# A two-block transformer kernel: modulation columns moved into the state-space stage, one weight bank fetched early, expert slots by one-hot products

## Time and profile before

| | |
|---|---|
| median of 3 runs | 5024.47 us (5023.44 to 5026.74) |
| profiled execution | 5026.53 us, its span 5024.3 us |
| PE busy | 4302.4 us (86%) |
| DVE busy | 3027.8 us (60%) |
| ACT busy | 1993.8 us (40%) |
| POOL busy | 292.2 us (6%) |
| DMA | 700.93 MB, mean 140 GB/s |

### The profile page before, as it was taken

The page is one execution under the profiler, slowest core; times in us unless marked ns, Lnnn a source line. Parts: engine busy times, 40 slices in busy tenths (PEclk is TensorE's granted clock), DMA queues, the critical chain, the costliest instruction groups (busy, mean ns, idle before and its releaser), DMA issues. The chain is left out here.

```text
span 5024.3 us, 60591 instructions
## 1 busy us (share of the span) xinstructions
PE 4302.4 (86%) x21370; PEld 3341.1 (66%) x21370; DVE 3027.8 (60%) x3938; ACT 1993.8 (40%) x3109; POOL 292.2 (6%) x197
## 2 busy tenths in 40 slices
PE   7999699999675987999799999997597399999960
PEld 5777489888564865888555555555476278787740
DVE  6676455555465763444555555556654489888856
ACT  3344233333112543322233333333321277777743
POOL 0000110000000000000100000000000311111112
PEclk9999799999787998999899999998799699999985
DMA  4443411111563325222600000008443388888957
GB/s 170 144 147 129 151 52 39 39 39 44 170 195 130 109 86 180 70 68 65 196 13 13 13 19 13 13 5 258 171 137 108 122 312 316 314 319 331 392 202 285
DMA packets 345002, 700.93 MB, mean 140 GB/s; under 512 B 70816, under 2 KB 227488, under 8 KB 326432
## 3 DMA queue, kind: packets, MB, share of 16 engines
q1 hardware_dynamic: 312096, 608.98, 34.7%
q0 software_dynamic: 14848, 50.36, 2.7%
q10 hardware_dynamic: 17920, 39.85, 2.4%
HBM read 585.02 MB, written 194.56 MB: 155 GB/s over the span
## 5 line engine op out<-in xcount | busy, mean ns | idle before, releaser
L2189 DVE TENSOR_REDUCE a_part<-a_pA 128x1 f32<-128x1024 f32 (+1 forms) x384 | 360.8, 953 | 390.6 <-PE a_pA L2090 390.5
L2123 PE MATMUL a_pO<-a_PT,a_V 128*128 128x512 f32 x1152 | 587.7, 592 | 0.0
L2159 ACT ACTIVATE a_PT<-a_pB 128x512 f32<-128x512 f32 x576 | 343.9, 597 | 579.7 <-PE a_pB L2113 579.7
L2112 PE MATMUL a_pB<-a_QA,a_KH 128*128 128x512 f32 x576 | 458.0, 795 | 0.7 <-ACT a_QA L2151 0.7
L955 DVE TENSOR_REDUCE a_maxima<-a_pS 128x1 f32<-128x512 f32 x256 | 176.6, 690 | 177.3 <-PE a_pS L863 176.7
L3205 DVE TENSOR_TENSOR e_gate_low<-e_gate_w,e_gate_high 128x4096 fp32r<-128x4096 f32 x48 | 212.1, 4418 | 64.9 <-ACT e_gate_high L3137 64.6
L895 PE MATMUL a_pO<-a_V,a_PT 128*128 128x128 f32 x2048 | 249.4, 275 | 0.3 <-DVE a_PT L968 0.3
L895 PEld LDWEIGHTS a_pO<-a_V,a_PT 128*128 128x128 f32 x2048 | 243.4, 192 | 6.0 <-DVE a_PT L968 0.6
L2090 PE MATMUL a_pA<-a_KH,a_QA 128*128 128x512 f32 (+1 forms) x640 | 203.8, 385 | 50.4 <-DVE a_part L2189 30.4
L2123 PEld LDWEIGHTS a_pO<-a_PT,a_V 128*128 128x128 f32 x1152 | 205.6, 188 | 42.7 <-issue 1.0
L930 ACT ACTIVATE a_PT<-a_pT 128x512 f32<-128x512 f32 x128 | 69.5, 595 | 413.3 <-PE a_pT L881 413.3
(11 more groups left out here) (529 smaller groups left out, 9600.7 us busy)
## 6 DMA issues: line engine op xcount, KB each, us to landing
e_gate_w<-in_moe_w_gate SPq DMA_DIRECT2D x49, 2048.0 KB
e_up_w<-in_moe_w_up SPq DMA_DIRECT2D x48, 2048.0 KB, 13.4
e_down_w<-in_moe_w_down SPq DMA_DIRECT2D x47, 2048.0 KB
between_yb<-e_Y SPq DMA_DIRECT2D x47, 512.0 KB, 7.9
between_x<-m_X SPq DMA_DIRECT2D x32, 512.0 KB, 3.0
r_W<-in_w_ada SPq DMA_DIRECT2D x8, 2048.0 KB, 22.3
between_yb<-a_zeros SPq DMA_DIRECT2D x31, 512.0 KB, 10.4
between_tv<-p_OV SPq DMA_DIRECT2D x16, 576.0 KB, 2.8
```

The costliest lines, as they stand in the source:

```text
L2112: pe.matmul(pB[t % 2][:], KH[g][:, tile], QA1[i % 2][:, heads, :], start=True, stop=False)
L2123: pe.matmul(pO[u % 2][:], V1[:, j, u % HKV, :], PT[:, t % RING, :], start=j == 0, stop=j == KT2 - 1).then_inc(S["o_ps"], 1)
L2159: act.activation(PT[:, t % RING, :], pB[t % 2][:], ACT.Exp, scale=scale).then_inc(S["p_ready"], 1)
L2189: dve.tensor_reduce(part[:, h, r % (NG2 // G4):r % (NG2 // G4) + 1], src, AX_X, ALU.max).then_inc(S["maxed"], 1)
```

## The change

- `modulations` is gone. Its work is in `s5`: piece p is multiplied in turn h = p + 1, between `states(h + 1, 0..3)` and `outputs(h)`, and turned after `outputs(h)`, through two more uses of the banks `pW`. ACT moves row and columns and issues the 2 MB load of the next piece; there is one buffer for pieces. The silu is made in turn 0: a tanh on ACT behind the first load, three operations on DVE behind `scan(0)`. Bias and gains are made by DVE after the last scan.
- Bank 0 of `w_in_2` is loaded by SP during tile 4 of `mix_1` into a tensor that both stages share.
- The scatter to `slots` is gone. The slots are now a tensor on chip, made as a sum of 32 products of one-hot matrices: `in_row` (which row of its block a pair has) by `in_block` (which block, times the token number). The weights `gate` and `up` of the first block are loaded by SP inside `dispatch`, before its end. The DVE operations of the places and of the blocks change order.
- `experts` has no `IDX` loads. POOL gathers from the slots on chip, in an unrolled loop, and waits for `t_ps` itself.

```diff
-def s5(nc, I, D, C):
+def s5(nc, I, D, C, M):
+        ada_w = k.sb("ada_w", [P, KC, BANK])
+        FIRST_PIECE = 2
+        def piece_of(h):
+            return h - FIRST_PIECE if FIRST_PIECE <= h < FIRST_PIECE + PIECES else None
+        def uses_before(h):
+            return USES * h + 2 * max(0, min(h - FIRST_PIECE, PIECES))
...
+            for dst, name in ((cc, "c2"), (b_col, "b_ada_col"), (g1, "g1")):
+                sp.dma_start(dst[:], I[name]).then_inc(S["c_vectors_loaded"], 16)
...
+            def modulation_row(h):
+                p, n = piece_of(h), uses_before(h) + USES
+                if p == 0:
+                    pe.wait_ge(S["cs_ready"], 1)
+                weights_free(n)
+                pe.wait_ge(S["ada_loaded"], 16 * (p + 1))
+                for c in range(KC):
+                    mm = pe.matmul(pW[n % 2][:], both[:, c].rearrange("p x y -> p (x y)"), ada_w[:, c, :], start=c == 0, stop=c == KC - 1)
+                mm.then_inc(S["w_ps"], 1)
+            def modulation_columns(h):
+                n = uses_before(h) + USES + 1
+                pe.wait_ge(S["w_moved"], n)
+                for m in range(4):
+                    tr = pe.transpose(pW[n % 2][:, m * P:(m + 1) * P], row[:, m * P:(m + 1) * P], C["ident"][:])
+                tr.then_inc(S["w_ps"], 1)
...
                     for j in range(4):
                         states(h + 1, j)
+                    if piece_of(h + 1) is not None:
+                        modulation_row(h + 1)
                 pe.wait_ge(S["products_1"], h + 1)
                 outputs(h)
+                if h + 1 < TURNS and piece_of(h + 1) is not None:
+                    modulation_columns(h + 1)
...
+            def load_piece(p):
+                src = I["w_ada"].rearrange("(k p) n -> p k n", p=P)[:, :, p * BANK:(p + 1) * BANK]
+                act.dma_start(ada_w[:], src).then_inc(S["ada_loaded"], 16)
+            def move_row(h):
+                n = uses_before(h) + USES
+                act.wait_ge(S["w_ps"], n + 1)
+                act.activation(row[:], pW[n % 2][:], ACT.Copy).then_inc(S["w_moved"], 1)
+                if piece_of(h) + 1 < PIECES:
+                    load_piece(piece_of(h) + 1)
...
                     move_weights(h + 1)
+                    if piece_of(h + 1) is not None:
+                        move_row(h + 1)
                 move_outputs(h)
+                if h + 1 < TURNS and piece_of(h + 1) is not None:
+                    move_columns(h + 1)
+                if h == 0:
+                    load_piece(0)
+                    act.wait_ge(S["c_vectors_loaded"], 48)
+                    act.activation(half_c[:], cc[:], ACT.Tanh, scale=0.5).then_inc(S["tanh_done"], 1)
...
 # mix_1, SP
+                if 4 <= i < 4 + EARLY:
+                    load_projection(i - 4)
...
 # project_2, SP
-            for n, (lo, hi) in enumerate(BANKS2):
+            for n in range(EARLY, len(BANKS2)):
...
 # dispatch, SP
+            sp.wait_ge(S["first_known"], 1)
+            first = sp.value_load(M["block_expert"][0:1, 0:1], min_val=0, max_val=NE - 1)
+            for n in ("gate", "up"):
+                src = I["moe_w_" + n].rearrange("e (p k) n -> p e (k n)", p=P)
+                sp.dma_start(M["W"][n][0][:].unsqueeze(1), src[:, ds(first, 1), :]).then_inc(S["w_loaded"], 16)
+            sp.wait_ge(S["w_loaded"], 32)
...
 # dispatch, PE
+            pe.wait_ge(S["tokens_in"], 1)
+            for q in range(4):
+                pe.wait_ge(S["rows_in"], q + 1)
+                for j in range(8 * q, 8 * q + 8):
+                    mm = pe.matmul(ps[:, 0:NBT], in_row[:, j, :], in_block[:, j, :], start=j == 0, stop=j == 2 * NT - 1)
+            mm.then_inc(S["listed"], 1)
...
 # dispatch, DVE, behind the places and blocks
+            do(dve.tensor_scalar(of_block[:], dest[:], 1 / P, 0.5 / P - 0.5, ALU.mult, ALU.add))
+            do(dve.tensor_scalar(of_block[:], of_block[:], ROUND, None, ALU.add))
+            do(dve.tensor_scalar(of_block[:], of_block[:], ROUND, None, ALU.subtract))
+            do(dve.scalar_tensor_tensor(of_row[:], of_block[:], -float(P), dest[:], ALU.mult, ALU.add))
+            tt(in_block[:], bcast(flat(of_block).unsqueeze(2), shape), bcast(blocks_c[:].unsqueeze(1), shape), ALU.is_equal)
             for n in range(2):
+                d = dve.tensor_tensor(in_block[:, n * NT:(n + 1) * NT, :], in_block[:, n * NT:(n + 1) * NT, :],
+                                      bcast(token[:].unsqueeze(2), [P, NT, NBT]), ALU.mult)
+            for q in range(4):
+                dve.tensor_tensor(in_row[:, js, :], bcast(flat(of_row)[:, js].unsqueeze(2), [P, 8, P]), bcast(rows[:].unsqueeze(1), [P, 8, P]),
+                                  ALU.is_equal).then_inc(S["rows_in"], 1)
+            do(dve.tensor_copy(M["slots"][:], ps[:, 0:NBT]))
-                for t in range(NT):
-                    pool.indirect_dma_start(out=D["slots"], out_offset=bass.IndirectOffsetOnAxis(ap=M["dest"][:, n, t:t + 1], axis=0),
-                                            in_=token[:, t:t + 1], in_offset=None).then_inc(S["scattered"], 16)
...
 # experts, SP
-            load_indices(tile_at(0))
-            load_indices(tile_at(1))
-            load("gate", tile_at(0))
-            load("up", tile_at(0))
...
 # experts, POOL
+            for i in range(NB + 1):
+                if i >= 2:
+                    pool.wait_ge(S["t_ps"], i - 1)
+                pool.indirect_dma_start(out=XG[i % 2][:], out_offset=None, in_=D["h"],
+                                        in_offset=bass.IndirectOffsetOnAxis(ap=M["slots"][:, i:i + 1], axis=0)).then_inc(x_loaded[i % 2], 16)
```

More of the change, by code:

```diff
@@ L1062, in s5 @@
         Y = [k.sb(f"Y{b}", [P, HG, NCH]) for b in range(2)]
+        ada_w = k.sb("ada_w", [P, KC, BANK])
+        cc, half_c = (k.sb(n, [P, KC, 2]) for n in ("cc", "half_c"))
+        both = k.sb("both", [P, KC, 2, P // 2])
+        row = k.sb("row", [P, BANK])
+        columns = k.sb("columns", [P, PIECES, 4, 2])
+        b_col, g1 = k.sb("b_col", [P, NMOD * KC]), k.sb("g1", [P, KC])
         pW = [k.ps(f"pW{b}") for b in range(2)]
@@ L1288, in waiting_sp, with mix_1 @@
     return wait
-def mix_1(nc, I, D, C):
+def mix_1(nc, I, D, C, M):
     with ExitStack() as ctx:
@@ L1368, in tile @@
                     load(Tile(t.i + 2, t.b, t.n + 1))
-            tiles(sp, NT, tile, last=3)
+            tile(tile_at(0))
+            for i in range(1, NT):
+                tile(tile_at(i))
+                if 4 <= i < 4 + EARLY:
+                    load_projection(i - 4)
             store(tile_at(NT - 1))
@@ L1899, in _ @@
                 act.wait_ge(w_loaded[n], 16)
[L1900 removed]
+                act.activation(WH[:, :, lo:hi], low_part(n).bitcast(F32), ACT.Copy).then_inc(S["w_high"], 1)
             tiles2(act, tile)
@@ L2824, in dispatch @@
         upper = k.sb("upper", [P, P])
-        token = k.sb("token", [P, NT], I32)
-        zero_i = k.sb("zero_i", [P, NBT], I32)
-        pw, pt = k.ps("pw"), k.ps("pt")
-        names = "loaded exp1_in exp1 exp2_in exp2 step chosen ranks zeroed filled placed scattered".split()
+        token, rows = k.sb("token", [P, NT]), k.sb("rows", [P, P])
+        of_block, of_row = k.sb("of_block", [P, 2, NT]), k.sb("of_row", [P, 2, NT])
+        in_block = k.sb("in_block", [P, 2 * NT, NBT])
+        in_row = k.sb("in_row", [P, 2 * NT, P])
+        pw, pt, ps = k.ps("pw"), k.ps("pt"), k.ps("ps")
+        names = "loaded exp1_in exp1 exp2_in exp2 step chosen ranks first_known w_loaded tokens_in rows_in listed".split()
         S = {n: k.sem(n) for n in names}
@@ L3008, in tile @@
                 i = t.i
-                wait(S["t_ps"], i + 1)
-                load_indices(Tile(i + 2, t.b, t.n + 1))
                 load("down", t, None if t.first else i)
@@ L3019, in skipped @@
                 i = t.i
-                wait(S["t_ps"], i + 1)
-                sp.sem_inc(i_loaded[t.b], 16)
                 wait(w_low["down"], i)
@@ L3378, in block_pair_kernel @@
         attention_1(nc, I, C, D)
-        s5(nc, I, D, C)
-        mix_1(nc, I, D, C)
-        modulations(nc, I, D, C, M)
-        project_2(nc, I, D, C, M)
+        s5(nc, I, D, C, M)
+        with ExitStack() as projection:
+            early = Kit(nc, projection, "p2w")
+            M["w_in_2"] = early.sb("w_in_2", [P, KC, BANKS2[EARLY - 1][1]], F32R)
+            M["w_in_2_loaded"] = [early.sem(f"loaded{n}") for n in range(EARLY)]
+            mix_1(nc, I, D, C, M)
+            project_2(nc, I, D, C, M)
         attention_2(nc, C, D)
@@ L3392, in block_pair_kernel @@
         mix_2(nc, I, D, C, M)
-        dispatch(nc, I, D, C, M)
-        experts(nc, I, D, C, M)
+        M["slots"] = k.sb("slots", [P, NBT], I32)
+        with ExitStack() as weights:
+            raw = Kit(nc, weights, "w")
+            M["W"] = {n: [raw.sb(f"{n}{b}", [P, KC * DE]) for b in range(2 if n == "up" else 1)] for n in ("gate", "up", "down")}
+            dispatch(nc, I, D, C, M)
```

(1 more changed line is left out.)

195 lines of the change are left out of this document (70 added, 125 removed).

## The result

The kernel after takes 4964.8 us (median of 4 runs, 4963.92 to 4967.69) against 5023.95 (5019.85 to 5026.74) for the kernel before beside it: ratio 0.9884, 95% interval 0.9872 to 0.9896. The forecast was 4958.0, its range 4942 to 4982. The profiled executions have spans of 5024.3 and 4962.3 us, 62.0 apart.

| stretch | before to after | forecast |
|---|---|---|
| state space, from the second move of outputs(0) to the mixing stage's first issue | +37.5 | +33.0 |
| everything between, mixing stage | +0.6 | 0 |
| last store of the mixing stage to the projection's first issue (the modulations lay there) | -44.5 | -44.0 |
| projection, first issue to first product | -1.8 | -0.4 |
| retention stage, untouched | -3.2 | 0 |

A forecast was written before the change was run, and what follows sets the result against it. No engine was taken to bound the whole kernel, since barriers separate stages. Terms -44.0 + 33.0 - 0.4 - 36.5 + 0 - 18.6 = -66.5 us took the median 5024.5 to 4958 us, range 4942 to 4982.

The forecast's parts named there:

- Modulations' stage: Between mixing stage and projection: the whole stage goes, from 1880.79 to the projection's first issue at 1924.80, -44.0 us.
- State space: State-space stage: the modulations' work moved there is not hidden and adds +33.0 us together, bounds 30 and 38.
- The row: State space, on PE between states and outputs: 16 instructions of 0.43 us, 6.9 us a row, four times, +27.4 us.
- the load of piece 0: State space, turn 0: issued ahead of twelve loads, it fills the queue, +3.2 us including 0.4 for its issue.
- The columns: State space: four transposes and a small copy ahead of ACT's issues, about 0.6 us a turn, +2.4 us.
- the rows are covered: Rival, state space: PE's stand behind ACT's issues shrinks by the row's time, 24 us come back, 4934 us; chance 0.06.
- The cover that I counted for the silu: State space: the first row ahead of outputs(1) plus a 2.7 us margin covers states some 4 us late, by 9.6 us.
- Early bank: Projection's start: ACT's 0.36 us wait for bank 0 goes, the rest there being tile 0's normalisation, -0.4 us.
- Dispatch: Dispatch and first expert block: first product at 3945.8 against 3982.33, -36.5 us, bounds -38.2 and -31.2.
- 16 at the lower clock, 48 at the full: Dispatch, 64 one-hot instructions on PE after over 20 us idle: 9.2 us, bounds 7.5 and 14.5.
- Real blocks: Experts' real blocks: fewer waits in SP's queue within 11.6 us of idle time, taken as 0, bounds -4 and +3.
- Skipped blocks: Experts' skipped blocks: gather pairs 4.75 us apart, not 6.65, and a 7 us earlier start, -18.6 us.

The follow-up runs named there:

- loads alone: Kernel after without the modulations' row products, column transposes and their copies in the state space, the four loads kept: 4939.83 us.
- moved away: Kernel after with the first piece of modulation weights loaded by SyncE instead of ScalarE: 4951.24 us.
- the dummies: Kernel after with seven unread products of 512 columns on TensorE ahead of the one-hot products: 4963.85 us.
- the hop: Kernel after with GpSimd's gathers waiting for a semaphore that SyncE raises behind TensorE's transposes, first in SyncE's list for each block, no index load: 4963.07 us.

## Why the prediction was right, and where it was off

- **Modulations' stage**, -44.0: -44.5. Right.
- **State space**, +33.0: +37.5. The row was right (7.03 against 6.9, shown also by leaving it out), and so was its place on PE's path. The mis-sized term is the load of piece 0 in front of the twelve loads: I took 3.2 and it cost 6.6 (loads alone) to 7.1 (moved away), past my bound of 5.6 for it. The columns, for which I took 2.4, cost nothing that can be seen: four rows with their columns took 27.3 us, 29.8 in my sum. Another 3 us are in turns 4 to 6 of that profiled run, 29.2, 28.0 and 27.6 us. Of eight other runs with this same stage three had such turns (sum of the seven turns 228.8 to 229.1, one of them with its excess in turn 3), and five had 27.2 to 27.4 there and a sum of 225.8 to 226.1, which is +34.1 to +34.4. So the stage has two paces, and the ledger has the slower. The granted clock of turn 4 is 0.82 in the kernel after and 0.88 in a run with the shorter turns. Why it fell lower stays open.
- **The rival that the rows are covered** I gave 0.06, because ACT's issues begin behind the outputs and the stand moves along. That was right for this placement. What I did not ask is whether the row could move into the stand: it can, for nothing in turns 1 to 3. The cover that I counted for the silu (9.6 us) goes with that move: in turn 0 2.7 us of it then show.
- **Early bank**, -0.4: -1.8. The step was "ACT waited 0.36 us for bank 0". I read the visible wait as all of it, and missed that a table load stood in front and would go too.
- **Dispatch**, -36.5: -32.4. The failed step is "16 at the lower clock, 48 at the full": all 64 ran at the lower. 9.2 became 13.89, inside my bound of 14.5, and the dummies show the clock as cause. The other steps held within 1 us. That an instruction of 65 columns would cost what one of 36 does was right: 0.217 and 0.113 us against the 0.227 and 0.117 that I took.
- **Real blocks**, 0: -1.4, and right only as a sum. Under it lie two effects that I named in one clause and did not price. The shortest step between two tanhs fell from 17.7 to 17.3 us, but PE's wait for the hidden part rose from 7.7 to 22.8 us (15.8 to 24.1 over the runs with this gather), as I read it because the gathers now meet the down and up loads. Three runs that put the gather elsewhere take 9 to 15 us off against the runs on their chips; on a third chip the same steps took 8 to 10 us less without any such edit. That nothing there "can be worth more than the 11.6 us left" was wrong as well: 832.4 is 14.5 us below the 846.9 that the same steps took before. PE's busy time, whose ends are modelled, is no floor.
- **Skipped blocks**, -18.6: -15.4, and -10.3 to -13.7 in six other runs. Pairs of 4.9 for my 4.75 (4.6 to 6.0 over all runs), and a smaller head start. The mis-sized step is the landing: I took the 4.5 us of before, and without the hop the median was 5.2 to 5.4 where the traces have it. (Six pairs at 1.9 are also 11.4 and not the 11.6 of my sum.) That the detour over SyncE and the gather set the pace is shown by the hop (+5.5 to +10.6) and by leaving the gather out (-13.9 to -19). By the Trainium skill (DMA: Bandwidth & Descriptors, the anatomy of one DMA on the SWDGE path) the gathers would land in 3.2 us, an estimate from its figures, and the pairs would be 3.5 apart. The traces show medians of 4.3 to 5.4 us for a landing and no pair under 4.6, so they do not agree, and the measurement decides.
- **Retention**, untouched: -3.2 of the ledger. From its first small load to its last store it took 150.5 us before, 147.4 after, and 147.3 to 150.5 in four of the experiments, none of which touches it. It is the spread of that stage, and no part of the change.
- **The range**. My bounds for the single terms add up to 4946 and 4983, not to the 4942 and 4978 that I wrote; the result lies well inside either. That it comes within 7 us of the forecast is in part luck, since misses of both signs cancel: 4.5 us in the state space, 4.1 in dispatch and 3.2 in the skipped blocks on the one side, and on the other 1.4 each in projection and real blocks and the 3.2 of the retention stage, which nobody forecast.

## What to carry to other kernels

A piece of work that is moved onto a busy engine belongs into the stand that this engine has anyway, not beside it: the same row cost 7.0 us in front of the outputs and nothing between two transposes. A transfer freed from a wait starts at another moment, so look at which transfers it then meets; here that seems to have taken back most of what the shorter queue gave the real blocks. A wait that the profile shows is only the last of several: behind a table load and 0.36 us stood 1.42.

## What was not expected of the hardware

- 64 instructions (32 products) of 65 columns, run without a gap for 13.9 us, never raised the granted clock from 0.50; 14 instructions of 512 columns before them had it at 1.00 for their whole stretch, at half the time for each (0.113 against 0.217 us).
- Filling its stand made PE's turn shorter than without the extra work (26.94 against 27.4 us, granted clock 1.00 against 0.88).
- A load of 2 MB ahead of twelve others in one engine's queue made the issue of eight of them take 10.2 us in place of 7.3, and the engine's own work stood for it; on SyncE's queue the same load left it at 7.8 us, and the turn was no longer than its neighbours.
